# Seventeen convolution taps in an attention loop: bursts at four ticks, or one tap a tick

## The reference

```python
p = h @ w_in[l]
u_val, u_gate, g_conv, c_q, c_kv, k_idx, w_idx, g_attn = jnp.split(p, offsets, axis=-1)
y_conv = conformer_conv(u_val, u_gate, ...) * jax.nn.silu(g_conv)
y_attn = dsa_attention(c_q, c_kv, k_idx, w_idx, ...) * jax.nn.silu(g_attn)
y = jnp.concatenate([y_conv, y_attn], axis=-1) @ w_out[l]
x = x + gate[:, None, :] * rmsnorm(y, g_post[l])
```

## Time and profile before

| what | value |
|---|---|
| time, median of three runs | 1806.3 us (1804.48 to 1809.34) |
| profiled execution: its time / its span | 1804.48 us / 1803.1 us |
| PE busy | 1644.6 us, 91% |
| DVE busy | 729.7 us, 40% |
| ScalarE busy | 477.8 us, 26% |
| GpSimd busy | 312.3 us, 17% |
| mean granted TensorE clock | 0.948 |
| line 2440 (taps), both layers | 60 scalar_tensor_tensor, mean 869 ns |
| line 2672 (GpSimd's sums) | 180, mean 1112 ns |

### The profile page before, as it was taken

The page is one execution under the profiler, slowest core; times in us unless marked ns, Lnnn a source line. Parts: engine busy times, 40 slices in busy tenths (PEclk is TensorE's granted clock), DMA queues, the critical chain, the costliest instruction groups (busy, mean ns, idle before and its releaser), DMA issues.

```text
span 1803.1 us, 15312 instructions
## 1 busy us (share of the span) xinstructions
PE 1644.6 (91%) x5832; PEld 810.8 (45%) x5832; DVE 729.7 (40%) x1519; ACT 477.8 (26%) x979; POOL 312.3 (17%) x312
## 2 busy tenths in 40 slices
PE   6999999999989698888788887999999999999998
PEld 3544445655454343333333332544455544445553
DVE  2626524445143421110011011549975143998522
ACT  2013233101030110000000000546466234645631
POOL 0000000100000111211111010138324012751600
PEclk9899999999999899989889898999999999899999
DMA  8321031455353579999999998600302130030101
GB/s 325 140 93 47 1 116 49 171 200 194 110 208 122 228 308 403 408 406 407 403 410 405 400 413 350 251 0 24 105 13 89 47 111 0 0 117 24 47 1 47
DMA packets 70960, 324.30 MB, mean 180 GB/s; under 512 B 9290, under 2 KB 12626, under 8 KB 58464
## 3 DMA queue, kind: packets, MB, share of 16 engines
q1 hardware_dynamic: 63552, 308.03, 43.9%
q0 software_dynamic: 6016, 10.51, 1.8%
q10 hardware_dynamic: 1312, 4.72, 0.7%
HBM read 318.95 MB, written 12.67 MB: 184 GB/s over the span
## 4 chain that ended last, share of the span: by engine, by line
PE 68%; DMA 19%; DVE 9%; ACT 2%; issue 2%; POOL 0%; SPq 0%; ACTq 0%; DVEq 0%; POOLq 0%
PE bank L187 65%; DMA arena<-in_w 15%; DMA arena<-h_rows,arena 3%; DVE arena L2456 1%; DVE arena L1214 1%; PE bank L2055 1%; DVE arena L2510 1%; PE bank L567 1%; DVE arena L2497 0%; DVE arena L2512 0%; DVE bank L2488 0%; PE bank L875 0%; DVE arena L2440 0%; DMA arena<-in_params 0%; PE bank L662 0%
## 5 line engine op out<-in xcount | busy, mean ns | idle before, releaser
L187 PE MATMUL bank<-arena 128*128 128x512 f32 (+11 forms) x4964 | 1540.9, 549 | 93.6 <-DMA arena<-in_w 56.4
L187 PEld LDWEIGHTS bank<-arena 128*128 128x128 f32 (+3 forms) x4964 | 707.0, 180 | 859.6 <-issue 790.7
L2672 POOL TENSOR_TENSOR arena<-arena 128x512 f32<-128x512 f32 x180 | 200.2, 1112 | 214.8 <-ACT arena L2281 198.0
L1763 POOL TENSOR_TENSOR arena<-arena 128x1 f32<-128x1 f32 (+2 forms) x44 | 32.4, 738 | 684.0 <-DVE arena L1204 459.1
L1711 DVE TENSOR_TENSOR arena<-arena,bank 64x512 f32<-64x512 f32 x32 | 22.1, 691 | 313.7 <-ACT arena L1170 313.7
L2281 ACT ACTIVATE arena<-arena 128x512 f32<-128x512 f32 x180 | 126.1, 717 | 20.1 <-POOL arena L2672 19.9
L1170 ACT ACTIVATE arena<-bank 64x512 f32<-64x512 f32 x32 | 18.9, 591 | 377.4 <-PE bank L187 377.4
L959 ACT COPY arena<-bank 128x512 f32<-128x512 f32 (+3 forms) x114 | 60.9, 540 | 218.4 <-PE bank L187 134.0
L1784 POOL DMA_INDIRECT y_rows<-arena x32 | 32.1, 1004 | 411.4 <-PE bank L875 275.1
L1705 DVE COPY arena<-bank 128x512 f32<-128x512 f32 x32 | 22.2, 692 | 113.5 <-PE bank L875 113.5
L1214 DVE SCALAR_TENSOR_TENSOR arena<-arena 128x512 f32<-128x512 f32 x84 | 63.2, 752 | 3.0
(11 more groups left out here) (264 smaller groups left out, 870.0 us busy)
## 6 DMA issues: line engine op xcount, KB each, us to landing
arena<-in_w SPq DMA_DIRECT2D x96, 2048.0 KB, 35.2
arena<-in_w_in SPq DMA_DIRECT2D x15, 2048.0 KB, 10.8
arena<-in_w_ada SPq DMA_DIRECT2D x12, 2048.0 KB, 8.9
arena<-in_w_out SPq DMA_DIRECT2D x6, 2048.0 KB, 7.7
arena<-in_w_xk SPq DMA_DIRECT2D x2, 2048.0 KB, 9.2
arena<-in_w_xv SPq DMA_DIRECT2D x2, 2048.0 KB, 8.2
arena<-in_w_xq SPq DMA_DIRECT2D x2, 2048.0 KB, 9.9
arena<-in_w_xo SPq DMA_DIRECT2D x2, 2048.0 KB, 9.0
```

Of the source, the lines that this page charges most:

```text
L187: i = pe.e.matmul(o, l, r, start=first and j == 0, stop=last and j == len(pairs) - 1)
L2672: pool.e.tensor_tensor(yc, yc, k.prod[l][n % 4], ALU.add).then_inc(*k.pool.step("sum", l, f, j))
```

## The change

The table `TAPS_AT` goes. In its place DVE issues one tap behind each tick, from tick 13 (`TAP_AT`) on, until the 31 are done. With 14 taps ahead of the loop these are ticks 13 to 29. The order of the taps, what each computes, and all other engines' programs stay as they are.

```diff
-PROD_AT, TAPS = 8, 14
-TAPS_AT = {1: 5, 5: 5, 10: 4, 24: 3}
+PROD_AT, TAP_AT, TAPS = 8, 13, 14
...
-        if tick in TAPS_AT:
-            dve_taps(k, dve, l, tap, tap + TAPS_AT[tick])
-            tap += TAPS_AT[tick]
+        if TAP_AT <= tick < TAP_AT + 31 - tap:
+            dve_taps(k, dve, l, tap + tick - TAP_AT, tap + tick - TAP_AT + 1)
```

## The result

The changed kernel takes 1819.33 us (median of 4 runs, 1817.05 to 1822.27) against 1805.99 us before. The ratio is 1.0069, with a 95% interval of 1.0055 to 1.0084: 0.7% slower. I had forecast 1820.3 us.

The account below looks back on a forecast made before the run. TensorE was taken as the bound, VectorE following closely; spread taps make VectorE the bound. 6.0 us before the last g_conv block plus 1.0 behind it, 7.0 a layer, 14.0 in both, gave 1820.3 us; range 1811 to 1836.

Parts of the forecast that it names:

- The bursts cost nothing, and their removal gives back nothing: Ticks 1, 5, 10 and 24: all 17 taps there were hidden, so removing them gives back 0.
- VectorE bounds the stages of ticks 13 to 23: Attention loop before the last g_conv block: VectorE's work delays TensorE's transposes of tick 24 by 6.0 us a layer.
- The taps' own time: Lower bound with no GpSimd collision: 2.8 us a layer, nothing behind the g_conv block, 1812 us.
- Collisions: VectorE and GpSimd block each other: 0.75 us each, two a stage without gate product, half of one with it.
- Stage 9: Two-tick loop stage without gate product: 1.27 + 1.40 + 1.50 = 4.17 us.
- Stage 8: Two-tick loop stage with gate product: 3.74 us, the odd tap and its collision filling 1.45 of TensorE's 2.24.
- stage 10: Two-tick loop stage with gate product: 3.41 us, TensorE's 1.79 filled by odd tap, collision, bias add and reciprocal.
- Behind the g_conv block: Taps after the loop's last g_conv block: 1.0 us a layer lost, and the loss stays.
- The granted clock: Rival: TensorE's clock halves in the loop, six us a layer more; 1826.5 with one layer, 1832.5 both; chance 0.32.
- Few collisions: Rival: VectorE and GpSimd fall in step, loss 3 to 4.5 us a layer, 1812 to 1815; chance 0.14.
- no change: Rival: VectorE's waits in the loop hold the taps, 1806 us; chance 0.06.
- faster: Rival: the burst of tick 5 holds up TensorE today; gain 3.1 us a layer, 1800; chance 0.03.

Follow-up runs that it names:

- the odd and even placements: Changed kernel with its 17 loop taps mostly in twos, behind odd ticks only (13 to 29) or even ticks only (14 to 30): 1819.32 us and 1834.06 us.
- the clock kept full: Changed kernel with one extra unused TensorE product at ticks 14, 16, 18, 20, 22, 26 and 28: 1819.23 us.
- short sums: GpSimd's 30 sums in the loop cut to one of 512 columns: 1812.12 us on the changed kernel, 1801.01 us on the kernel before.

## Why the prediction came out right

Its mechanism and its time were right; several terms were not, and they made up for each other. That the sum came out within 0.3 us a layer is in part luck.

- **The bursts cost nothing, and their removal gives back nothing.** Shown: without any tap in the loop it is as long as before, 82.78 us.
- **VectorE bounds the stages of ticks 13 to 23.** Shown by the waits that end with its normalization, and by the odd and even placements. I had 6.0 us a layer there. The runs had 7.0 and 6.6, and 6.4 with the clock kept full (1344.40 to 1363.82, 19.42 us).
- **The taps' own time.** The bound without a collision was 2.8 us; measured 2.7, over a base that held 0.8 us of collisions itself.
- **Collisions.** 3.2 us by my count in this stretch; measured 3.7 (19.42 − 15.70). By stage they lay elsewhere. Stage 9 (1351.15 to 1354.03) took 2.88 us where I had 4.17, with no collision at a tap. Stage 8 (1346.95 to 1351.15) took 4.20 where I had 3.74, with one of 0.9 us at the even tap. The largest miss is stage 10 (1354.03 to 1359.47): 5.44 us where I had 3.41. 0.9 of it is the fall of the clock. For the rest I had filled the wait for the gate product with a collision of the odd tap; that tap met no sum, and 0.84 us of wait was left even at full clock. My rule of two collisions a stage without a gate product and a half with one was wrong in place and right in sum, which is luck.
- **Behind the g_conv block.** The mis-sized term: 1.0 us a layer forecast, 0.3 measured. The 1.0 up to stage 13 was right (1370.77 to 1380.18 is 9.41, before 8.38), but I wrote that the loss stays because nothing is changed behind it. It doesn't: in the kernel before a later normalization started behind one of GpSimd's sums and took 1.30 us, and in the changed kernel that of the same stage started ahead of one and took 0.48 (rows below). So the shift of VectorE against GpSimd's sums removed it. With short sums the same 0.8 us went from the kernel before.
- **The granted clock.** I held its fall for a rival of 6 us a layer with a chance of 0.32. It fell, in both layers of the profiled run, and cost 0.6 and 0.2 us net, at most 0.9 for one fall. The error is the price: PE at half speed is partly hidden where VectorE is the bound, and a fall shows whole only on a block that PE bounds, 1.7 us in the even version. That no fall met the g_conv block here is luck too: the second one ended at 1362.22, and the block began at 1362.57. The falls also explain a sign that I had given wrongly: PE's idle time in the stretch rose to 6.4 us and not to 8.5, since PE at half speed is busy for longer.
- **Few collisions; no change; faster.** The first was half true of stages and false of the sum. The other two are excluded by the interval, the last also by the run without taps.

The sum and the normalization behind the g_conv block, in order of time, of the kernel before and then of the changed kernel:

```profile
1371.51 1.09 POOL L2672 TENSOR_TENSOR arena<-arena 128x512 f32<-128x512 f32 x1 [0.23 <-ACT arena L2281]
1371.58 1.30 DVE L2510 TENSOR_SCALAR arena<-arena 128x512 f32<-128x512 f32 x1
```

```profile
1381.16 0.48 DVE L2508 TENSOR_SCALAR arena<-arena 128x512 f32<-128x512 f32 x1
1381.29 1.30 POOL L2669 TENSOR_TENSOR arena<-arena 128x512 f32<-128x512 f32 x1
```

The sum, in the measured terms of layer 0: 7.0 up to the block, 0 in it, 1.0 behind up to stage 13, less 0.8 after it: 7.3 by the trace, of which the rounded terms give 7.2. Forecast: 6.0 + 1.0 = 7.0. With 6.9 in layer 1 the loops lost 14.2 us where I had 14.0.

## What to carry to other kernels

Filler work for an engine that follows closely belongs in one piece under a block of another engine that it doesn't feed. Spread evenly it looks gentler, but each piece stands ahead of something that the bounding engine waits for, and here 11 pieces of 0.7 us cost 7 us. If it must be spread, put it behind the instruction that releases the bound, not ahead: the same 17 taps cost 6.2 us behind odd ticks and 14.0 behind even ones, 1.7 of it a fall of the clock on the g_conv block. And take the neighbour on the shared port into the count, in the kernel before as well: what seemed a tight schedule held 3 us a layer of collisions, which moving GpSimd's sums only shifted to other places.

## What the runs showed of the hardware

A tap that met a GpSimd sum took up to 1.65 us (at 1348.10 above) against 0.74, so it waited up to 0.9 us and not the 1.09 us that a sum takes. The Trainium skill (SBUF — State Buffer, SBUF: two separate sides) has the later of the two blocked until the first is finished. The trace agrees that they hold each other up, with a shorter wait, and in both directions: a sum that started at 1351.66, behind a tap of 1351.55, took 1.57 us.

The granted clock fell to 0.50 after PE had been kept waiting by VectorE (2.15 us ahead of the transposes at 1350.71, then 0.50 in the stretch 1352.00:1355.40), and not after each such wait: it stayed at 1.00 in the middle of the changed kernel with short sums, where PE waited too. With an extra product in each stage it was 1.00 in both layers' loops. What a fall costs depends on where it lies: 1.7 us on a block that PE bounds, 0.4 to 0.9 where VectorE is the bound.
